# Decay masks in spare rows of the one-hot products, and weight slot 0 for few blocks only

## The chip, the cores and the metric

One core of one Trainium2 chip runs the kernel. The metric is the device time of one execution in microseconds; three runs of the kernel before gave 1845.36 to 1845.75, median 1845.67.

## The reference

A sequence of 256 tokens of width 1024 goes through two blocks of two layers each, all in float32. A layer of the first block is an FFN, a mixer and a second FFN; a layer of the second block is a hybrid layer of attention and a gated recurrence. The change lies in the mixer, whose state-space part works in chunks of 128 tokens, in both directions, for 16 heads:

```python
def ssd_chunked(x, dt, a, bm, cm):
    ...
    a_cs = jnp.cumsum(dtc * a, axis=2)
    seg = a_cs[:, :, :, None] - a_cs[:, :, None, :]
    lower = jnp.tril(jnp.ones((L, L), dtype=bool))[None, None, :, :, None, None]
    decay = jnp.exp(jnp.where(lower, seg, -jnp.inf))
    cb = jnp.einsum('bclgn,bcsgn->bclsg', cc, bc)
    y_diag = jnp.einsum('bclsg,bclsgr,bcsgrp->bclgrp', cb, decay, xd)
    ...
```

For each head, chunk and direction a 128 x 128 tile `exp(a_cs[l] - a_cs[s])` is needed, zero where s is later than l (or earlier, for the reversed direction). All other work of the change concerns the weight matrices of every projection: `x @ w` for FFNs (`w_gate`, `w_up`, `w_down`), mixers (`w_in`, `mla_w_uq`, `mla_w_ukv`, `w_out`) and hybrid layers.

## The kernel before

**Weights.** All weight matrices are cut into 586 blocks, mostly of 128 partitions x 1024 values (two 128-row pieces of the contraction, 512 columns). SyncE (SP) loads block j into a raw slot, ScalarE copies it to a rounded high part (`WH`, five buffers, j % 5), VectorE subtracts and writes the low part (`WL`) over the raw block in place. TensorE then makes three passes of fp32r products: left high by weight high, left low by weight high, left high by weight low. Products of a projection are of kind "feat" (a feature block: weights are the stationary operand, 24 products of 256 columns per block, in three thirds of 8) or "tok" (a token block: weights move, 12 products of 512 columns). The last block of a projection runs half by half. `split_of` (L1054) gives block j raw slot j % 8: slots 1 to 7 lie side by side in `RAW`/`WL`, slot 0 is a tensor of its own, `RAW0`/`WL0`, that starts at a multiple of 512 bytes, where the others don't. In its program SP waits for the end of block j - 8 before it loads block j into the slot; ScalarE's `split` (L1592) waits for the load and for the end of block j - 5, whose `WH` buffer it reuses.

**Order.** A planner in Python, the class `Order`, writes one list of phases ("block", "seg", "flip", "cum" and so on) ahead of time, and each engine runs the phases that concern it, in that order, with semaphore waits between engines. The planner has a cost for every phase (`WORK`: "P53" is 0.53 us on TensorE, A is ScalarE, V VectorE, G GpSimd) and puts phases and weight blocks where its clock says that they fit. Generators say what a phase must come after (`yield "ex", i` waits, `yield [("cum", i)]` emits).

**The mixer's decay tiles.** `cum` (TensorE L1350, ScalarE L1819, VectorE L2415) makes the cumulated logarithms by fp32 products over `DA` and `LN` and leaves them in `LBH`, 128 rows x 512: rows 0 to 15 hold one value per head with sign for the "to" side, rows 64 to 79 for the "from" side, rows 32 to 47 and 96 to 111 the low parts of the same; other rows are zero. `ex` makes exponentials from `DA`, too. `seg` (TensorE L1416) builds one PSUM bank of four 128 x 128 tiles (two directions, two heads) with five products: the mask first, the identity by `CUT` (0 or -1e30, the two directions repeated for two heads, 512 columns); then for each head a one-hot column of `TO`, repeated 128 times with step zero as the stationary operand, by 256 columns of `LBH`; then for each direction 128 columns of `LBH` by one-hot columns of `FROM`, repeated with step zero. There are 16 `seg` per mixer. ScalarE takes the exponential (`ET`), VectorE adds the directions and multiplies by C and B, and `apply` multiplies by the values with plain fp32 products. Plain fp32 products show as two matmul records each.

The heads of the mixer's attention (`sc`, `pt`, `pv`) run before; `heads()` waits for `ex`, and the tiles begin when `mo_a` of the second half is emitted. `QTQ` and `QTK` (queries and keys, at the bottom of the arena) are read last by `sc` of heads 6 and 7. `mo_var` on GpSimd is an inverse root for the attention's output norm. `cn_a` belongs to the mixer's convolution branch and stands behind the first two tiles; its PSUM bank is that of the first tile.

Of the kernel before, what the change touches and what calls it, by code (L numbers as in the profile page):

```python
# [6 lines left out]
F32 = mybir.dt.float32  # L7
F32R = mybir.dt.float32r
# [12 lines left out]
BLK = 1024  # L21
HALF = 3.1415925
STAGES = [("ffn", 0, 1), ("mix", 0), ("ffn", 0, 2), ("ffn", 1, 1), ("mix", 1), ("ffn", 1, 2),
          ("hyb", 0), ("hyb", 1)]
# [32 lines left out]
def constants():  # L57
# [22 lines left out]
    r = np.concatenate([eye, fwd, bwd, pick.reshape(128, 32)], 1)  # L80
    return np.ascontiguousarray(c, np.float32), g, r


# [70 lines left out]
class Lin:  # L154
# [88 lines left out]
class Order:  # L243
# [307 lines left out]
    def mix(self, i, l):  # L551
# [25 lines left out]
        def decay():  # L577
            yield "evict", ("sm", i)
            for x in range(4):
                yield [("decay", i, x)]  # L580
            yield "kpe", i
            for t in range(2):
                yield "lat_y", i, t
            yield [("cum", i)]
            yield [("ex", i)]

# [33 lines left out]
        def heads():  # L620
            for t in range(2):
                yield "qk_rope", i, t
            yield "ex", i
            yield "evict", ("xbc", i, 1)
            yield [("qkt", i, g) for g in range(0, 8, 2)]
            yield [("qkt", i, g) for g in range(8, 16, 2)]
            yield [("tbanks", (0, 1, 3)), ("heads", i)]
            for h in range(2):
                self.go(mla_head(h))
            yield "pv", i, 7  # L630
            yield [("mo_a", i, 1), ("tbanks", (2, 3))]
            yield [("mo_sq", i, t) for t in range(2)]
            yield [("mo_var", i, t) for t in range(2)]
            yield [("mo_y", i, t) for t in range(2)]
            yield [("flip", "mo", i, c, 2) for c in (8, 10)]
# [231 lines left out]
class Kernel:  # L867


    def __init__(self, nc, ctx, io, order):  # L870
        self.nc, self.ctx, self.io = nc, ctx, io
        self.sig = Signals(nc, ctx)
        self.order = order
        self.blocks, self.lins = order.blocks, order.lins
        self.w_at, at = [], 0
        for lin, kk, _, _ in self.blocks:
            self.w_at.append(at)
            at += 128 * len(kk) * lin.w
        self.bank, self.stats, self.stat_at = {}, {}, {}
        self.allocate()  # L880

    def fixed(self, name, shape, dt=F32):
# [21 lines left out]
    def allocate(self):  # L904
# [55 lines left out]
        self.LN, _ = mk("LN", [128, 2, 2, 128], m)  # L960
        self.MPT, m = mk("MPT", [128, 2, 2, 256], m)
        self.DA, m = mk("DA", [128, 2, 2, 128], m)
        self.DT, m = mk("DT", [128, 2, 32], m)
# [16 lines left out]
        assert x <= p2  # L980
        self.LBH, x = mk("LBH", [128, 512], p1, F32R)
        self.ET, _ = mk("ET", [128, 4, 512], 32768)
# [71 lines left out]
    def split_of(self, j):  # L1054

        lin, kk = self.blocks[j][:2]
        size = len(kk) * lin.w
        n = j % NRAW
        raw, lo = (self.RAW[:, n - 1, :], self.WL[:, n - 1, :]) if n else (self.RAW0[:, :], self.WL0[:, :])
# [60 lines left out]
class PE:  # L1120
# [229 lines left out]
    def cum(self, i):  # L1350
        k, w = self.k, self.w
        b, ps = self.tbank(("cum", i), "cum_dve", i)
        w.wait_ge(*self.at("const6", 0))
        w.wait_ge(*self.at("decay_dve", (i, 3)))
        w.wait_ge(*self.at("decay_act", (i, "ln")))
# [7 lines left out]
    def ex(self, i):  # L1363
        k = self.k
        b, ps = self.tbank(("ex", i), "ex_act", i)
        for t in range(2):
            for d in range(2):
# [48 lines left out]
    def seg(self, i, n):  # L1416
# [5 lines left out]
        w.wait_ge(*self.at("cum_dve", i))  # L1422
        w.wait_ge(*self.at("const5", 0))
        self.mm(ps, k.EYER, k.CUT.unsqueeze(2).to_broadcast([128, 2, 2, 128]), True, False)
        h0 = 8 * g + 2 * q
        for x in range(2):
            self.mm(ps[:, :, x, :], k.TO[:, h0 + x:h0 + x + 1].to_broadcast([128, 128]),
                    k.LBH[:, 256 * t:256 * t + 256].rearrange("p (d s) -> p d s", d=2), False, False)
        for d in range(2):
            m = self.mm(ps[:, d, :, :], k.LBH[:, 256 * t + 128 * d:256 * t + 128 * d + 128],  # L1430
                        k.FROM[:, h0:h0 + 2].unsqueeze(2).to_broadcast([128, 2, 128]), False, d == 1)
        m.then_inc(*self.up("seg_pe", (i, n)))
# [123 lines left out]
class Scalar:  # L1556
# [35 lines left out]
    def split(self, j):  # L1592
# [4 lines left out]
        if j == 0:  # L1597
# [4 lines left out]
            return  # L1602
        w.wait_ge(*self.at(f"raw{j % NRAW}", j))
        if j >= NSPLIT:
# [214 lines left out]
    def cum(self, i):  # L1819
# [4 lines left out]
        for t in range(2):  # L1824
            w.wait_ge(*self.at("lat_act", (i, t, "y")))
        self.act(k.LBH[:, :], ps[:, :], ACT.Copy).then_inc(*self.up("cum_act", i))

# [155 lines left out]
class Vector:  # L1983
# [431 lines left out]
    def cum(self, i):  # L2415
        k, w, e = self.k, self.w, self.e
        ps = k.PS[k.bank["cum", i]]
        w.wait_ge(*self.at("cum_act", i))
        e.tensor_tensor(k.LBH[32:64, :], ps[32:64, :], k.LBH[32:64, :].bitcast(F32), ALU.subtract)
        e.tensor_tensor(k.LBH[96:128, :], ps[96:128, :], k.LBH[96:128, :].bitcast(F32), ALU.subtract).then_inc(*self.up("cum_dve", i))  # L2420

# [323 lines left out]
class Pool:  # L2745
# [6 lines left out]
    def program(self):  # L2752
        do = {
            "setup": self.setup, "setup2": self.setup2, "rstd": self.rstd, "mix_pads": self.mix_pads,
            "lat_var": self.lat_var, "kpe": self.kpe, "qk_sum": self.qk_sum, "mo_var": self.mo_var,
            "fin_var": self.fin_var, "hyb_load": self.hyb_load,
            "hq_sum": self.hq_sum, "hb_sum": self.hb_sum, "oan_var": self.oan_var,
# [53 lines left out]
    def qk_sum(self, i, t):  # L2811
# [3 lines left out]
        for name, n in (("k", 8), ("q", 0)):  # L2815
            self.e.tensor_tensor(st[:, n:n + 8], st[:, n:n + 8], k.HM[:, 0:8], ALU.pow).then_inc(*self.up("rsqrt_pool", (name, i, t)))

    def mo_var(self, i, t):
        self.rsqrt(("mo", i, t), 8)
# [22 lines left out]
class Sync:  # L2842
# [6 lines left out]
    def program(self):  # L2849
# [10 lines left out]
        for j, (lin, kk, _, _) in enumerate(k.blocks):  # L2860
            at, size = k.w_at[j], len(kk) * lin.w
            if j < 2:
                continue
            if j >= NRAW:
                w.wait_ge(*self.at("block", j - NRAW))
            e.dma_start(k.split_of(j)[0], k.io["WALL"][at:at + 128 * size].rearrange("(p n) -> p n", p=128)).then_inc(
                *k.sig.landed(f"raw{j % NRAW}", j))
        for n in range(2):
# [30 lines left out]
def pack_small(inputs):  # L2899
# [6 lines left out]
    for name, n in ROWS:  # L2906
        for l in range(L):
# [3 lines left out]
            "ROWP": np.ascontiguousarray(np.concatenate(rows, 1)), "CST": c,  # L2911
            "CSTG": g, "CSTR": r,
            "x": np.asarray(inputs["x"]), "POSITIONS": np.ascontiguousarray(
# [30 lines left out]
```

## Time and profile before

| | us |
|---|---|
| median of three runs | 1845.67 |
| the profiled execution, its own time | 1845.08 |
| its span, first to last instruction | 1843.3 |
| TensorE busy | 1828.3 |
| VectorE busy | 1266.7 |
| ScalarE busy | 1055.9 |
| GpSimd busy | 100.5 |

The profile is one execution. TensorE's granted clock is 1.000 of full speed over it. Matmuls overlap in their pipeline and their ends are modelled, so a matmul's recorded duration is longer than its share of time; the distance from one start to the next is what it costs. The timeline merges neighbours of one kind and writes how many ("x8"). On GpSimd the records are rough. DMA queues are listed by the engine that issues: SPq for the weights, POOLq for constants.

### The profile page before, as it was taken

To read this page: it belongs to the slowest core of one execution; us is meant where nothing else is said; L and a number is where in the kernel's file an instruction comes from. 1 tells how busy PE (TensorE), PEld (TensorE's weight loads), DVE (VectorE), ACT (ScalarE), POOL (GpSimd) and SP (SyncE) were. 2 spreads that over 40 slices of the span, in tenths; PEclk is the share of its full clock that TensorE was granted. 3 is DMA by queue.
4 is the path that set the end of the run, shared out by engine and by line. 5 is a ranking of instruction groups with operands and counts; after the bars stand their busy time and mean duration, and the time that the engine had idled before them with its cause. 6 is when DMAs were issued, how large, how long until landed. Compare 5 with 4: busy or idle time off the path is not lost.

```text
span 1843.3 us, 28625 instructions
## 1 busy us (share of the span) xinstructions
PE 1828.3 (99%) x11626; PEld 1628.1 (88%) x11626; DVE 1266.7 (69%) x1944; ACT 1055.9 (57%) x1557; POOL 100.5 (5%) x85
## 2 busy tenths in 40 slices
PE   9999999999999999999999999999999999999999
PEld 9998998789998999899789998988878888887887
DVE  6764797766665665588876665687667567875755
ACT  6444767565444444576755544475776456568642
POOL 0000110000000000020000000002001000210100
PEclk9999999999999999999999999999999999999999
DMA  8555542345555556553325555554445555534553
GB/s 292 193 191 182 188 151 100 106 137 189 192 193 186 190 195 194 180 179 112 126 92 172 191 193 189 173 184 147 139 137 182 194 163 182 171 126 137 172 192 116
DMA packets 86596, 310.09 MB, mean 168 GB/s; under 512 B 9648, under 2 KB 10288, under 8 KB 86464
## 3 DMA queue, kind: packets, MB, share of 16 engines
q1 hardware_dynamic: 85680, 306.35, 50.7%
q8 instruction: 92, 1.51, 0.3%
q0 software_dynamic: 496, 1.65, 0.2%
q14 instruction: 40, 0.33, 0.1%
q10 hardware_dynamic: 288, 0.25, 0.0%
HBM read 307.16 MB, written 1.05 MB: 167 GB/s over the span
## 4 chain that ended last, share of the span: by engine, by line
PE 95%; ACT 3%; DVE 1%; issue 0%; DMA 0%; POOL 0%; SPq 0%; DVEq 0%; ACTq 0%
PE bank L1162 92%; PE bank L1159 3%; ACT PA L1579 1%; DVE PA L2686 0%; ACT MP L1579 0%; ACT WH L1579 0%; ACT L1579 0%; DVE WL L2034 0%; DMA X<-in_x_dram 0%; ACT ET L1579 0%; DVE PC L2711 0%; DVE STATS L2384 0%; ACT BZ L1579 0%; DVE BO L2676 0%; DVE X L2120 0%
## 5 line engine op out<-in xcount | busy, mean ns | idle before, releaser
L2034 DVE TENSOR_TENSOR WL<-RAW,WH 128x1024 fp32r<-128x1024 f32 x585 | 704.6, 1213 | 405.0 <-ACT WH L1579 403.4
L1579 ACT ACTIVATE WH<-RAW 128x1024 fp32r<-128x1024 f32 (+2 forms) x587 | 610.1, 1050 | 497.0 <-PE bank L1162 494.2
L1162 PE MATMUL bank<-WH,FR 128*128 128x512 f32 x1264 | 318.4, 390 | 0.0
L1162 PEld LDWEIGHTS bank<-WH,FR 128*128 128x128 f32 x1264 | 233.7, 188 | 48.4 <-issue 0.8
L1162 PE MATMUL bank<-XTH,WH 128*128 128x256 f32 x1792 | 254.4, 279 | 0.6 <-ACT XTH L1579 0.6
L1162 PE MATMUL bank<-XTH,WL 128*128 128x256 f32 x1792 | 251.9, 278 | 0.0
L1162 PE MATMUL bank<-XTL,WH 128*128 128x256 f32 x1792 | 251.1, 277 | 0.0
L1162 PEld LDWEIGHTS bank<-XTH,WH 128*128 128x128 f32 x1792 | 226.9, 188 | 1.5 <-issue 0.8
L1162 PEld LDWEIGHTS bank<-XTH,WL 128*128 128x128 f32 x1792 | 226.7, 188 | 0.0
L1162 PEld LDWEIGHTS bank<-XTL,WH 128*128 128x128 f32 x1792 | 226.0, 188 | 0.0
L1162 PE MATMUL bank<-WL,FR 128*128 128x512 f32 x632 | 173.7, 389 | 0.0
L1162 PE MATMUL bank<-WH,XTHS 128*128 128x512 f32 x576 | 165.0, 398 | 0.0
L1162 PE MATMUL bank<-WL,XTHS 128*128 128x512 f32 x576 | 160.7, 390 | 0.0
L1162 PE MATMUL bank<-WH,XTLS 128*128 128x512 f32 x576 | 160.3, 390 | 0.0
L1162 PEld LDWEIGHTS bank<-WL,FR 128*128 128x128 f32 x632 | 118.4, 188 | 24.9
L1162 PEld LDWEIGHTS bank<-WH,XTLS 128*128 128x128 f32 x576 | 108.1, 188 | 23.2
L1162 PEld LDWEIGHTS bank<-WL,XTHS 128*128 128x128 f32 x576 | 108.1, 188 | 23.1
L1162 PEld LDWEIGHTS bank<-WH,XTHS 128*128 128x128 f32 x576 | 104.3, 188 | 21.4 <-issue 2.0
L2787 POOL TENSOR_TENSOR STATS<-STATS,HALFS 128x1 f32<-128x1 f32 (+2 forms) x36 | 68.0, 1900 | 662.0 <-DVE STATS L2593 174.2
L1579 ACT ACT_TABLE_LOAD x43 | 55.2, 1283 | 3.7 <-PEq L2935 1.7
L2219 DVE SCALAR_TENSOR_TENSOR XC<-XBG,COLP,XC 128x256 f32<-128x256 f32 x96 | 46.4, 484 | 8.5 <-ACT XC L1579 5.5
L1579 ACT ACTIVATE PA<-PA,STATS 128x128 f32<-128x128 f32 x64 | 34.2, 536 | 21.6 <-DVE STATS L2692 21.6
(337 smaller groups left out, 1850.6 us busy)
## 6 DMA issues: line engine op xcount, KB each, us to landing
RAW<-in_WALL_dram SPq DMA_DIRECT2D x569, 512.0 KB, 3.3
RAW<-in_WALL_dram SPq DMA_DIRECT2D x8, 448.0 KB, 3.3
RAW<-in_WALL_dram SPq DMA_DIRECT2D x8, 256.0 KB, 2.6
X<-in_x_dram SPq DMA_DIRECT2D x4, 256.0 KB, 5.5
out_dram<-X SPq DMA_DIRECT2D x4, 256.0 KB, 2.0
ROWP<-in_ROWP_dram POOLq DMA_DIRECT2D x1, 672.0 KB, 11.0
CONSTS<-in_CST_dram POOLq DMA_DIRECT2D x1, 664.0 KB, 7.9
ROUNDED<-in_CSTR_dram POOLq DMA_DIRECT2D x1, 208.0 KB, 12.2
```

The lines of the kernel that those rows point to most:

```text
L1159: return self.e.transpose(out, in_, self.k.EYE[0:rows, 0:rows])
L1162: return self.e.matmul(out, lhs, rhs, start=start, stop=stop, skip_group_check=True)
L1579: return self.e.activation(out, in_, func, **k)
L2034: self.e.tensor_tensor(lo, raw, hi.bitcast(F32), ALU.subtract).then_inc(*self.up("lo", j))
L2219: e.scalar_tensor_tensor(o, src[:, tap:tap + 256], k.col("ssd_conv_w", l, 12 * tap + ch), o, ALU.mult, ALU.add).then_inc(*self.up("conv_dv ...
L2787: self.e.tensor_tensor(st, st, k.HM[:, 0:n], ALU.pow).then_inc(*self.up("rsqrt_pool", key))
```

## The change

Mask: the 64 free rows of the one-hot operands are filled. Each half of a mask (two -1e30 triangles) is written as a sum over 64 runs of neighbouring columns, so the one-hot matrix holds the runs and the other operand's free rows hold the cut for each run; the four one-hot products then add the mask as well, and the fifth product, the mask itself, is gone. For this the one-hot operands become real 128 x 128 matrices, one per head: `TOX` and `FROMX` (1,024 KB each), at the bottom of the arena in the room of `QTQ` and `QTK`, and the values are kept in two tiles, `LBT` (values in rows 0 to 63, cuts below) and `LBF` (cuts above, values in rows 64 to 127), the latter in the room of `DA`. A new phase `scan_load` on GpSimd loads the two matrices and the two cuts (128 KB each) in every mixer, once the scores of heads 6 and 7 and `cum` have been made. `ex` comes before `cum`, since `LBF` overwrites `DA`; `heads()` waits for `cum`. ScalarE evicts `cum` in two copies of 64 partitions.

Slots: `place_blocks` decides each block's raw slot. It collects rows of "feat" blocks of FFNs and mixers that follow each other with no other work of TensorE between them. Slot 0 goes to a block only if its last use is at least 7 blocks ago, the block isn't the last of its row, the row hasn't had it yet, and the block isn't the last of its projection; every other block takes the longest unused of slots 1 to 7. SP waits for the block that had the slot before.

```diff
+        used, self.slot, self.before = [-NRAW] * NRAW, [], []
+        for j in range(len(self.blocks)):
+            row = rows.get(j, [j])
+            if not j or (j - used[0] >= NRAW - 1 and j != row[-1] and used[0] not in row and not self.blocks[j][3]):
+                n = 0
+            else:
+                n = min(range(1, NRAW), key=lambda s: used[s])
+            self.slot.append(n)
+            self.before.append(used[n])
+            used[n] = j
...
-        n = j % NRAW
+        n = self.slot[j]
...
-            if j >= NRAW:
-                w.wait_ge(*self.at("block", j - NRAW))
+            if k.before[j] >= 0:
+                w.wait_ge(*self.at("block", k.before[j]))
...
-    "cum": "P198 A60 V140", ... "seg": "P53 A61 V90",
+    "cum": "P198 A105 V140", ... "seg": "P32 A61 V90",
...
+            yield [("ex", i)]
             yield [("cum", i)]
-            yield [("ex", i)]
...
-            yield "ex", i
+            yield "cum", i
...
-            yield [("mo_a", i, 1), ("tbanks", (2, 3))]
+            yield [("mo_a", i, 1), ("scan_load", i), ("tbanks", (2, 3))]
...
     def seg(self, i, n):
...
-        w.wait_ge(*self.at("const5", 0))
-        self.mm(ps, k.EYER, k.CUT.unsqueeze(2).to_broadcast([128, 2, 2, 128]), True, False)
+        w.wait_ge(*self.at("scan_in", i))
         h0 = 8 * g + 2 * q
         for x in range(2):
-            self.mm(ps[:, :, x, :], k.TO[:, h0 + x:h0 + x + 1].to_broadcast([128, 128]),
-                    k.LBH[:, 256 * t:256 * t + 256].rearrange("p (d s) -> p d s", d=2), False, False)
+            self.mm(ps[:, :, x, :], k.TOX[:, h0 + x, :], k.LBT[:, 256 * t:256 * t + 256].rearrange("p (d s) -> p d s", d=2),
+                    x == 0, False)
         for d in range(2):
-            m = self.mm(ps[:, d, :, :], k.LBH[:, 256 * t + 128 * d:256 * t + 128 * d + 128],
-                        k.FROM[:, h0:h0 + 2].unsqueeze(2).to_broadcast([128, 2, 128]), False, d == 1)
+            m = self.mm(ps[:, d, :, :], k.LBF[:, 256 * t + 128 * d:256 * t + 128 * d + 128], k.FROMX[:, h0:h0 + 2, :], False, d == 1)
...
-        self.act(k.LBH[:, :], ps[:, :], ACT.Copy).then_inc(*self.up("cum_act", i))
+        self.act(k.LBT[0:64, :], ps[0:64, :], ACT.Copy)
+        self.act(k.LBF[64:128, :], ps[64:128, :], ACT.Copy).then_inc(*self.up("cum_act", i))
...
+    def scan_load(self, i):
+
+        k, w, e = self.k, self.w, self.e
+        for h in (6, 7):
+            w.wait_ge(*self.at("sc_pe", (i, h)))
+        w.wait_ge(*self.at("cum_pe", i))
+        w.wait_ge(*self.at("kpe_pool", (i, 1)))
+        src = k.io["CSTX"]
+        e.dma_start(k.TOX[:, :, :], src[:, 0:2048].rearrange("p (h s) -> p h s", h=16)).then_inc(*k.sig.landed("scan_in"))
+        e.dma_start(k.FROMX[:, :, :], src[:, 2048:4096].rearrange("p (h s) -> p h s", h=16)).then_inc(*k.sig.landed("scan_in"))
+        e.dma_start(k.LBF[0:64, :], src[0:64, 4096:4608]).then_inc(*k.sig.landed("scan_in"))
+        e.dma_start(k.LBT[64:128, :], src[64:128, 4096:4608]).then_inc(*k.sig.landed("scan_in", i))
```

## Rows read from the trace of the kernel before

**Rows 1.** busy time of each engine in the whole span (page, part 1)

```profile
PE 1828.3 (99%) x11626; PEld 1628.1 (88%) x11626; DVE 1266.7 (69%) x1944; ACT 1055.9 (57%) x1557; POOL 100.5 (5%) x85
```

**Rows 2.** groups of matmuls by shape: count, busy us and mean ns

```profile
L1162 PE MATMUL bank<-ROUNDED 128*128 128x512 f32 x32 | 14.9, 465 | 0.0
```

**Rows 3.** timeline of TensorE, `seg` 7 and `seg` 11: start us, us, operation

```profile
359.63 0.48 PE L1162 MATMUL bank<-ROUNDED 128*128 128x512 f32 x1
359.95 0.40 PE L1162 MATMUL bank<-LBH,ROUNDED 128*128 128x256 f32 x2
360.18 0.38 PE L1162 MATMUL bank<-ROUNDED,LBH 128*128 128x256 f32 x2
...
368.61 0.39 PE L1162 MATMUL bank<-ROUNDED 128*128 128x512 f32 x1
368.84 0.40 PE L1162 MATMUL bank<-LBH,ROUNDED 128*128 128x256 f32 x2
```

**Rows 4.** timeline of TensorE behind `rows` of the second layer's FFN

```profile
603.05 1.19 PE L1162 MATMUL bank<-XTH,WH 128*128 128x256 f32 x8
604.08 1.10 PE L1162 MATMUL bank<-XTL,WH 128*128 128x256 f32 x8
...
605.97 1.07 PE L1162 MATMUL bank<-XTH,WH 128*128 128x256 f32 x8
```

**Rows 5.** timeline of TensorE, feature blocks 127 to 130

```profile
423.05 1.10 PE L1162 MATMUL bank<-XTH,WH 128*128 128x256 f32 x8
...
425.88 1.10 PE L1162 MATMUL bank<-XTH,WH 128*128 128x256 f32 x8
...
428.71 0.62 PE L1162 MATMUL bank<-XTH,WH 128*128 128x256 f32 x4
...
431.43 0.39 PE L1162 MATMUL bank<-XTH,WH 128*128 128x256 f32 x2
```

**Rows 6.** timeline of TensorE at the first tiles of a mixer

```profile
340.97 0.49 PE L1162 MATMUL bank<-ROUNDED 128*128 128x512 f32 x1
...
343.07 0.67 PE L1162 MATMUL bank<-CHC,CONSTS 128*32 128x256 f32 x8 [0.29 <-ACT ET L1579]
```

**Rows 7.** timeline of ScalarE at the same place

```profile
341.13 1.28 ACT L1579 ACT_TABLE_LOAD   x1 [0.65 <-PE bank L1162]
342.42 1.09 ACT L1579 ACTIVATE ET<-bank 128x512 f32<-128x512 f32 x2
```

**Rows 8.** timeline of TensorE, feature blocks 136 and 137

```profile
447.75 1.07 PE L1162 MATMUL bank<-XTH,WH 128*128 128x256 f32 x8
...
450.53 0.62 PE L1162 MATMUL bank<-XTH,WH 128*128 128x256 f32 x4
```

**Rows 9.** timeline of TensorE, token blocks 168 to 170

```profile
535.03 1.98 PE L1162 MATMUL bank<-WH,FR 128*128 128x512 f32 x8
...
537.78 2.00 PE L1162 MATMUL bank<-WH,FR 128*128 128x512 f32 x8
...
540.52 1.98 PE L1162 MATMUL bank<-WH,FR 128*128 128x512 f32 x8
```

**Rows 10.** timeline of TensorE, the last scores of a mixer

```profile
292.86 1.03 PE L1162 MATMUL bank<-QTK,QTQ 96*128 96x256 f32 x4
```

**Rows 11.** DMA issues (page, part 6): count, KB each, us to landing

```profile
RAW<-in_WALL_dram SPq DMA_DIRECT2D x569, 512.0 KB, 3.3
...
ROWP<-in_ROWP_dram POOLq DMA_DIRECT2D x1, 672.0 KB, 11.0
```

**Rows 12.** stretch, length, busy us PE, PEld, DVE, ACT, POOL; clock, DMA share, GB/s

```profile
294.60:340.90 46.30, 45.71 (x242) 36.11 (x241) 37.11 (x55) 33.72 (x50) 3.34 (x2) 1.00 0.37 123
```

**Rows 13.** costliest groups (page, part 5): ScalarE's half of the weight split

```profile
L1579 ACT ACTIVATE WH<-RAW 128x1024 fp32r<-128x1024 f32 (+2 forms) x587 | 610.1, 1050 | 497.0 <-PE bank L1162 494.2
```

**Rows 14.** instructions on tile LBH: duration min/median/max ns

```profile
L2419 DVE TENSOR_TENSOR LBH<-bank,LBH x2: 683/683/683, 245.5 to 827.6; 32x512 fp32r<-32x512 f32 x2
```

**Rows 15.** timeline of TensorE, block 274, two behind slot 0

```profile
827.60 1.10 PE L1162 MATMUL bank<-XTH,WH 128*128 128x256 f32 x8
```

More of the change, by code:

```diff
@@ L22 @@
 HALF = 3.1415925
+ON_PE = set(("warm block flip rows cn_a cn_b qkt sc pt pv cum ex xs btk cbm state fin seg apply ift chain qkf msc mse mn "
+             "as at av").split())
 STAGES = [("ffn", 0, 1), ("mix", 0), ("ffn", 0, 2), ("ffn", 1, 1), ("mix", 1), ("ffn", 1, 2),
@@ L81, in constants, with scan_constants @@
     return np.ascontiguousarray(c, np.float32), g, r
+def scan_constants():
+    ends = [(1, 2)] + [(2 * j, 2 * j + 2) for j in range(1, 63)] + [(126, 127)]
+    i = np.arange(128)
+    runs = np.stack([(i >= a) & (i <= b) for a, b in ends]).astype(np.float32)
+    s = np.zeros((2, 128, 16, 128), np.float32)
+    for x in range(2):
+        for p in (64 * x, 64 * x + 32):
+            s[x, p + i[:16], i[:16]] = 1
+        s[x, 64 * (1 - x):64 * (1 - x) + 64] = runs[:, None, :]
+    cut = np.zeros((128, 2, 2, 128), np.float32)
+    for k, (a, b) in enumerate(ends):
+        cut[64 + k, :, 0] = np.where(i < a, -1e30, 0.0)
+        cut[64 + k, :, 1] = np.where(i > b, -1e30, 0.0)
+        cut[k, :, 0] = np.where(i > b, -1e30, 0.0)
+        cut[k, :, 1] = np.where(i < a, -1e30, 0.0)
+    return np.ascontiguousarray(np.concatenate([s[0].reshape(128, 2048), s[1].reshape(128, 2048), cut.reshape(128, 512)], 1))
 class Signals:
@@ L879, in __init__, with place_blocks @@
         self.bank, self.stats, self.stat_at = {}, {}, {}
+        self.place_blocks()
         self.allocate()
+    def place_blocks(self):
+        rows, alone = {}, True
+        for phase in self.order.phases:
+            if phase[0] not in ON_PE:
+                continue
+            j = phase[1]
+            if phase[0] != "block" or self.blocks[j][0].kind != "feat" or STAGES[self.blocks[j][0].key[1]][0] == "hyb":
+                alone = True
+                continue
+            row, alone = [] if alone else row, False
+            row.append(j)
+            rows[j] = row
+        used, self.slot, self.before = [-NRAW] * NRAW, [], []
[8 more added lines that the diff above has]
+            used[n] = j
     def fixed(self, name, shape, dt=F32):
@@ L961, in allocate @@
         self.MPT, m = mk("MPT", [128, 2, 2, 256], m)
+        self.LBF, _ = mk("LBF", [128, 512], m, F32R)
         self.DA, m = mk("DA", [128, 2, 2, 128], m)
@@ L980, in allocate @@
         assert x <= p2
-        self.LBH, x = mk("LBH", [128, 512], p1, F32R)
+        self.LBT, x = mk("LBT", [128, 512], p1, F32R)
+        self.TOX, _ = mk("TOX", [128, 16, 128], 0, F32R)
+        self.FROMX, _ = mk("FROMX", [128, 16, 128], 16384, F32R)
         self.ET, _ = mk("ET", [128, 4, 512], 32768)
@@ L1352, in cum @@
         b, ps = self.tbank(("cum", i), "cum_dve", i)
-        w.wait_ge(*self.at("const6", 0))
-        w.wait_ge(*self.at("decay_dve", (i, 3)))
         w.wait_ge(*self.at("decay_act", (i, "ln")))
@@ L1363, in ex @@
     def ex(self, i):
-        k = self.k
+        k, w = self.k, self.w
         b, ps = self.tbank(("ex", i), "ex_act", i)
+        w.wait_ge(*self.at("const6", 0))
+        w.wait_ge(*self.at("decay_dve", (i, 3)))
         for t in range(2):
@@ L1602, in split @@
             return
-        w.wait_ge(*self.at(f"raw{j % NRAW}", j))
+        w.wait_ge(*self.at(f"raw{k.slot[j]}", j))
         if j >= NSPLIT:
@@ L2418, in cum @@
         w.wait_ge(*self.at("cum_act", i))
-        e.tensor_tensor(k.LBH[32:64, :], ps[32:64, :], k.LBH[32:64, :].bitcast(F32), ALU.subtract)
-        e.tensor_tensor(k.LBH[96:128, :], ps[96:128, :], k.LBH[96:128, :].bitcast(F32), ALU.subtract).then_inc(*self.up("cum_dve", i))
+        e.tensor_tensor(k.LBT[32:64, :], ps[32:64, :], k.LBT[32:64, :].bitcast(F32), ALU.subtract)
+        e.tensor_tensor(k.LBF[96:128, :], ps[96:128, :], k.LBF[96:128, :].bitcast(F32), ALU.subtract).then_inc(*self.up("cum_dve", i))
     def state_x(self, i, d):
@@ L2755, in program @@
             "lat_var": self.lat_var, "kpe": self.kpe, "qk_sum": self.qk_sum, "mo_var": self.mo_var,
-            "fin_var": self.fin_var, "hyb_load": self.hyb_load,
+            "fin_var": self.fin_var, "hyb_load": self.hyb_load, "scan_load": self.scan_load,
             "hq_sum": self.hq_sum, "hb_sum": self.hb_sum, "oan_var": self.oan_var,
@@ L2863, in program @@
                 continue
-            if j >= NRAW:
-                w.wait_ge(*self.at("block", j - NRAW))
+            if k.before[j] >= 0:
+                w.wait_ge(*self.at("block", k.before[j]))
             e.dma_start(k.split_of(j)[0], k.io["WALL"][at:at + 128 * size].rearrange("(p n) -> p n", p=128)).then_inc(
-                *k.sig.landed(f"raw{j % NRAW}", j))
+                *k.sig.landed(f"raw{k.slot[j]}", j))
         for n in range(2):
@@ L2911, in pack_small @@
             "ROWP": np.ascontiguousarray(np.concatenate(rows, 1)), "CST": c,
-            "CSTG": g, "CSTR": r,
+            "CSTG": g, "CSTR": r, "CSTX": scan_constants(),
             "x": np.asarray(inputs["x"]), "POSITIONS": np.ascontiguousarray(
```

4 rows, old and new, of the table WORK are left out of this document.

## Prediction

> **What bounds the kernel now.** I read the busy table first: TensorE is busy for 1828.3 of 1843.3 us [rows 1], so work that it need not do is time saved, unless a wait grows in its place. The profiled execution took 1845.08 us for a span of 1843.3 us; the median of the runs is 1845.67 us, 0.6 above it. I make the sum on 1845.08 and add the 0.6 at the end. The busy times of overlapping matmuls are no pace, so every price of TensorE below is a distance from start to start in its timeline.
>
> **The mask matmul goes.** Each mixer builds 16 pairs of decay tiles (`seg`), and each `seg` begins with one 512-column matmul of the mask: 32 in all [rows 2]. What it takes depends on what ran before. Behind the plain-fp32 products of `apply` it is 359.95 - 359.63 = 0.32 us; behind another `seg` 368.84 - 368.61 = 0.23 us [rows 3]. The 0.09 between them isn't the mask's: the first fp32r matmul after plain-fp32 work pays it whatever it is (behind `rows` the first third of a block takes 604.08 - 603.05 = 1.03 us [rows 4], where a third of a block at the same pace takes 2.83 / 3 = 0.94 [rows 5]). The first one-hot product will pay it instead. So I take 0.23 a tile, with 0.32 as the other end.
>
> Not all 32 count. Behind the first two tiles of a mixer stands `cn_a`, which needs the bank of the first tile and so waits for its exponential [rows 6]; and that waits for an activation-table load from 341.13 to 342.41, whatever TensorE does [rows 7]. TensorE resumes at 343.07 as before. So 28 x 0.23 = **6.4 us**; the upper end is 28 x 0.32 = 9.0.
>
> The four products that remain keep their sizes, but read real matrices where they read one column at step zero. The trace has no such pair to compare. The nearest rows are the two paces of 256-column products over real matrices, 24 to a block: 2.72 / 24 = 0.113 and 2.83 / 24 = 0.118 us [rows 5]; today's take 360.18 - 359.95 = 0.23 for two [rows 3], in between. Ends for 128 products: -0.3 and +0.6 us; I take 0.
>
> **The slots.** Today every eighth block lies in slot 0 (RAW0/WL0), 74 of 586. The new rule gives it only to a block that isn't the last of its product, in an unbroken row of feature blocks of the FFNs and mixers, not at the row's end, once per row, and at least 7 blocks after its last use; a token block is a row of its own, so its own end, and never gets it. Counted along the block order of the trace, 14 are left. What slot 0 does stands in the timeline:
>
> Feature blocks run at 2.72 or at 2.83 us. A break (`rows`, transposes) sets the slow pace, and it stays until a block in slot 0 has passed: 2.83 from 423.05, the block in slot 0 from 425.88, then 2.72 [rows 5]. At the fast pace a block in slot 0 takes 450.53 - 447.75 = 2.78, and the pace stays fast [rows 8]. A token block takes 537.78 - 535.03 = 2.75 in slot 0 and the one behind it 540.52 - 537.78 = 2.74, where 2.72 is usual [rows 9].
>
> So, first, 43 token blocks leave slot 0, each worth 0.03 to 0.05 with its follower: **1.9 us**. Second, sixteen feature blocks in rows that are fast already leave it, four in each FFN: 16 x 0.055 = **0.9 us**. Third, the cure moves. By the rule it comes one block earlier at 71 (for 72), 87 (for 88) and 311 (for 312), two at 318 (for 320); rows that had none get one at 123, 189, 259, 268 and 275, with 2, 2, 3, 3 and 1 blocks behind it; 130 for 128 and 196 for 192 lose 2 and 4. Net 10 blocks x 0.11 = **1.1 us**. Three feature blocks of the hybrid layers leave slot 0 without gain, under 0.1 against. Together **3.8 us**.
>
> A rule of the Trainium skill speaks against this part. "SBUF — State Buffer", section "Who interferes with whom", gives TensorE two independent read ports, one for the moving operand and one for weights, and says that it never waits for anyone. By it the place of a weight block sets no pace and the part is worth 0. The trace disagrees: the same 24 products take 2.72, 2.78 or 2.83 us [rows 5, 8].
>
> **The scan load.** Four DMAs from POOL's queue, 2,304 KB per mixer, go out when the scores of heads 6 and 7 are done, at 293.9 [rows 10]. Behind them on POOL stands `mo_var` alone, which needs sums of heads that come later still; no weight load is in that queue. The first reader is `seg` 0 at 340.97 [rows 6], 47 us later. Bounds by the nearest loads: 512 KB in 3.3 us, and 672 KB in 11.0 us among others [rows 11], so 15 to 38 us. The DMA engines are 37% busy in that stretch [rows 12]. Hidden: 0. Without that cover each late us would be one of TensorE's, in both mixers. Weight loads that share the engines have room: ACT's split waited 494.2 us for TensorE to release a buffer [rows 13], not for data.
>
> **Seven slots in place of eight.** A load is then released by the end of block j-7. It lands 3.3 us later [rows 11], and the split waits for the end of block j-5 anyway, 2 x 2.72 = 5.4 us after the release. 0, by that margin of 2.1 us.
>
> **`ex` ahead of `cum`, and a copy in two.** The same products swap places. ACT copies twice 64 partitions, beside TensorE. On VectorE the two subtractions of `cum`, 0.68 us each [rows 14], come nearer to the rope of queries and keys, for which the heads' first transposes wait. Ends: 0, and 2 x 1.4 = 2.8 us if they push it in both mixers; the work ahead of that rope stays the same, so 0.
>
> **The planner** books `seg` at P32 in place of P53 and may interleave the output blocks otherwise. Each switch from plain fp32 to fp32r costs 0.09 [rows 3]; ten more or fewer per mixer are 1.8 us, either way. I take 0.
>
> **Sum.** 6.4 + 3.8 = 10.2; 1845.08 - 10.2 = 1834.9, on the scale of the median **1835.5 us**.
>
> **Rivals.**
>
> *The cure misses.* At block 272, behind `cum`, slot 0 did not cure: two blocks later a third still takes 1.10 us busy [rows 15], as at the slow pace, where the fast one has 1.07 [rows 5]. Today the next try comes 8 blocks later; with one try per row a miss lasts. Each FFN has one row of some 40 blocks, so a miss there costs 35 x 0.11 = 3.8 us. One gives 1839.3; from three on the kernel is slower than before (11.4 against 10.2), and four give 1850.7. Against it: behind `rows` it worked even at the head of a row (1.07 at 605.97 [rows 4]), and the four new places are inside theirs, as at 425.88. One miss 8%, more 3%, mostly all four, since they are alike.
>
> *The place of a block sets no pace:* what looks like the slot's doing comes from something else and stays: 1845.7 - 6.4 = 1839.3. For it: that one uncured case. 5%. The rule of the Trainium skill above would have it so.
>
> *The mask's time comes back as waits* for the exponentials or VectorE's two products per tile: 1845.7 - 3.8 = 1841.9. For it: the first pair of tiles does so today [rows 6, 7]. Against: each later pair has a weight block of 2.7 us between its `seg` and its `apply`. 6%.
>
> *The entry cost goes with the mask:* 9.0 in place of 6.4, 1832.9. 10%.
>
> *The load lands late:* from under 2,304 KB / 47 us = 49 KB per us on; the slower row moves 61. Ten us late in each mixer give 1855. 2%.
>
> **How the numbers follow.** The forecast has the remaining 66%. The range reaches below to the lost entry cost with a kind interleaving and quicker cures, 1830, and above to one miss with slow one-hot products, 1840.5; that leaves out less than 2 in 10. A measurement of this kernel can tell 0.2%, 3.7 us, from no change. Slower by more: four misses or a late load, 4%. Within: two or three misses, or the waits with a little more against them, 6%. Faster: 90%.
>
> **What would show it.** Right: the row of 32 mask matmuls is gone; from a `seg`'s first product to the next work it is 0.23 us shorter; TensorE's pause ahead of `cn_a` grows by 0.46; token blocks take 2.72 in unbroken rows; each FFN's long row turns from 2.83 to 2.72 once and never shows 2.78. Wrong: an FFN row at 2.83 to its end; TensorE waiting for the load at `seg` 0; one-hot products above 0.118; new waits for the exponentials; many blocks elsewhere in the order.

## The result, and the profile after

The kernel after takes 1848.30 us (median of 20, 1846.93 to 1850.96), the kernel before beside it 1845.49: a ratio of 1.0013, 95% interval 1.0007 to 1.0019. I had forecast 1835.5, in a range from 1830.0 to 1840.5. The time rose by 2.8 us where 10.2 were to go.

The profiled execution of after took 1848.81 us. Its first weight block starts at 9.84 us, that of before at 7.81; executions of one kernel differ by that much at the start (those of before lie at about 1845.2 or about 1847.4), so traces are compared from the first weight block on.

The parts of the change show as forecast. Of the kernel after: part 1 of the page (beside [rows 1]), the groups that replace the products over `LBH`, and DMA issues (columns as in [rows 11]):

```profile
PE 1824.0 (99%) x11594; PEld 1624.4 (88%) x11594; DVE 1266.7 (69%) x1944; ACT 1056.9 (57%) x1559; POOL 102.9 (6%) x93
...
L1211 PE MATMUL bank<-LBT,TOX 128*128 128x256 f32 x64 | 15.0, 316 | 0.2
L1211 PE MATMUL bank<-FROMX,LBF 128*128 128x256 f32 x64 | 12.7, 280 | 0.0
...
TOX<-in_CSTX_dram POOLq DMA_DIRECT2D x2, 1024.0 KB, 5.7
FROMX<-in_CSTX_dram POOLq DMA_DIRECT2D x2, 1024.0 KB, 7.6
```

The 32 mask matmuls of [rows 2] are gone, the scan load has landed 10 us after its first issue, where the first reader comes 50 us after it, and TensorE is busy 4.3 us less. Yet the span is 3.7 longer: what TensorE no longer does it now waits. Its waits that grew, first in after, then in before (us in total, times, longest):

```profile
PE bank L1211 <- DVE ET L2503: 3.6, 4, 1.1
...
PE bank L1208 <- ACT XS L1626: 2.0, 2, 1.0
...
PE bank L1211 <- ACT ET L1626: 1.0, 2, 0.5
...
PE bank L1162 <- ACT ET L1579: 0.6, 2, 0.3
...
PE bank L1159 <- ACT XS L1579: 0.5, 2, 0.3
```

In before TensorE waited for `ET` 0.6 us in all and never for VectorE's half of it. Cut into stages (from the start of a stage's first weight block in TensorE's timeline to that of the next stage), the six FFN and hybrid stages of after are 2.54 us shorter together, and the mixers longer: 216.13 to 218.82 and 216.49 to 218.04.

The reason stands in the list of phases. In each mixer the planner sorted everything behind `cum` and `ex` anew. Here are TensorE's phases of the decay tiles in both kernels (B is a weight block of `w_out`):

```
before: ... cn_b cn_b apply2 apply3 seg4 seg5 B apply4 seg6 apply5 seg7 B apply6 seg8 apply7 seg9
        cn_b cn_b apply8 apply9 seg10 seg11 B ... apply13 seg15 B flip flip apply14 apply15
after:  ... cn_b cn_b apply2 apply3 seg4 seg5 apply4 seg6 apply5 seg7 cn_b cn_b apply6 apply7
        seg8 seg9 B B apply8 seg10 apply9 seg11 B ... apply13 seg15 apply14 flip flip apply15
```

After spends a `w_out` block earlier, ahead of `seg` 0, and so has none between `seg` 5 and `apply` 4, nor behind `seg` 15. The timeline of TensorE in after, at `seg` 5 and at the end of the tiles, with the clock there (start, us, operation; in brackets idle time and what ended it; the windows have length, busy us of PE, PEld, DVE, ACT, POOL, granted clock, DMA share, GB/s):

```profile
359.42 0.40 PE L1211 MATMUL bank<-LBT,TOX 128*128 128x256 f32 x2
359.66 0.40 PE L1211 MATMUL bank<-FROMX,LBF 128*128 128x256 f32 x2
361.19 0.66 PE L1211 MATMUL bank<-XS,ET 128*128 128x64 f32 x4 [1.13 <-DVE ET L2503]
...
382.41 0.48 PE L1211 MATMUL bank<-LBT,TOX 128*128 128x256 f32 x2
382.73 0.40 PE L1211 MATMUL bank<-FROMX,LBF 128*128 128x256 f32 x2
383.82 0.66 PE L1211 MATMUL bank<-XS,ET 128*128 128x64 f32 x4 [0.69 <-DVE ET L2503]
385.46 1.94 PE L1208 MATMUL bank<-CONSTS,XS 128*128 128x128 f32 x8 [0.98 <-ACT XS L1626]
387.20 0.96 PE L1211 MATMUL bank<-XS,ET 128*128 128x64 f32 x4
...
384.00:386.00 2.00, 1.01 (x7) 0.91 (x8) 1.90 (x4) 2.00 (x3) 0.00 (x0) 0.81 0.01 2
386.00:388.00 2.00, 2.00 (x12) 2.00 (x10) 1.74 (x4) 1.66 (x5) 0.54 (x1) 0.50 0.03 8
```

At 361.19 `apply` 4 starts 1.3 us late: the tile must pass ScalarE's exponential and two products on VectorE first, and no block covers that. At 383.82 and 385.46 it happens twice in a row, and then the granted clock falls from 2.4 to 1.2 GHz: the eight transposes take 1.74 us from start to start, where they take 0.90 at 2.4 GHz (e11, below). The mean granted clock of after was below 1.000 in 19 of its 20 executions; before never shows that.

### The profile page after: what moved, and what is told of

Same layout as the page of the kernel before. It is cut to its first block, busy times and chain, and to the rows that moved or that the text cites. A ratio compares the mean times of both kernels' runs of the same rounds, so it can differ in the third digit from the quotient of the medians.

```text
span 1847.0 us, 28571 instructions
## 1 busy us (share of the span) xinstructions
PE 1824.0 (99%) x11594; PEld 1624.4 (88%) x11594; DVE 1266.7 (69%) x1944; ACT 1056.9 (57%) x1559; POOL 102.9 (6%) x93
## 4 chain that ended last, share of the span: by engine, by line
PE 90%; DVE 5%; ACT 4%; issue 1%; DMA 0%; POOL 0%; SPq 0%; DVEq 0%; ACTq 0%
PE bank L1211 87%; PE bank L1208 3%; DVE WL L2082 1%; ACT PA L1626 1%; ACT WH L1626 1%; DVE XC L2267 1%; DVE PA L2734 0%; DVE STATS L2386 0%; ACT MP L1626 0%; ACT L1626 0%; ACT ET L1626 0%; DMA X<-in_x_dram 0%; DVE XBG L2215 0%; DVE PC L2759 0%; DVE STATS L2432 0%
## 5 line engine op out<-in xcount | busy, mean ns | idle before, releaser
L1211 PEld LDWEIGHTS bank<-WH,XTHS 128*128 128x128 f32 x576 | 104.3, 188 | 20.9 <-issue 2.0
```

The lines of the kernel that those rows point to most:

```text
L1211: return self.e.matmul(out, lhs, rhs, start=start, stop=stop, skip_group_check=True)
```

## The experiments

Twelve kernels ran. The table has their medians beside the kernel before on the same chip, and from each trace the length against before's trace: the two mixers, the other six stages, and all from the first weight block on.

| kernel | median | before | mixers | others | sum |
|---|---|---|---|---|---|
| after | 1848.30 | 1845.49 | +2.69, +1.55 | -2.54 | +1.70 |
| e1 old order | 1840.49 | 1845.65 | -2.34, -2.16 | -2.18 | -6.68 |
| e2 swap alone | 1857.42 | 1845.65 | +5.84, +4.83 | -0.11 | +10.56 |
| e3 slots alone | 1843.57 | 1845.65 | -0.08, -0.50 | -2.10 | -2.68 |
| e4 mask alone | 1843.06 | 1845.65 | -0.93, -1.81 | +0.77 | -1.97 |
| e5 block up | 1852.07 | 1846.85 | +4.88, +3.61 | -2.64 | +5.85 |
| e6 bookings | 1847.48 | 1846.85 | +1.07, +1.34 | +0.50 | +2.91 |
| e7 no slot 0 | 1855.90 | 1846.85 | -1.94, -1.89 | +13.27 | +9.44 |
| e8 idle product | 1838.18 | 1846.85 | -2.28, -2.25 | -2.27 | -6.80 |
| e9 block early | 1845.07 | 1845.55 | +1.23, +0.89 | -2.57 | -0.45 |
| e10 mask and idle product | 1841.75 | 1845.55 | -2.17, -1.87 | +0.41 | -3.63 |
| e11 tail | 1846.00 | 1845.55 | +0.96, +0.55 | -2.17 | -0.66 |
| e12 all aligned | 1859.12 | 1845.55 | -0.47, -1.59 | +16.67 | +14.61 |

### The order against the parts

`e1_old_order`: after, with `Order` as before, and then

```diff
+        for i, st in enumerate(stages):
+            if st[0] == "mix":
+                self.phases.remove(("ex", i))
+                self.phases.insert(self.phases.index(("cum", i)), ("ex", i))
```

> The kernel after, with the list of phases of the kernel before: the planner books and sorts as before (cum ahead of ex, seg P53, cum A60), and ex is then moved up to stand just ahead of cum. Masks, loads and slots are those of after. Theory: the swap of ex and cum made the planner sort the rest of each mixer otherwise, and that order costs what the change was to bring; with the old order the mask and the slots bring their 6.4 and 3.8 us, so 1845.5 - 10.2 = 1835.3 (1834 to 1838). Rival: the new operands, their load or the slots cost it themselves, and the order is a bystander: about 1848, as after.

Measured: 1840.49, ratio 0.9968 (0.9956 to 0.9981). The rival falls: with the old order the same masks, loads and slots are faster than before. But 5.2 us came, not 10.2. The trace has 6.68; it is of the one execution of five whose mean granted clock was 1.000, and the fastest. What is missing from the forecast is taken apart below.

`e2_swap_alone`: before, with the two generator lines of the diff (`ex` yielded ahead of `cum`, `heads` waiting for `cum`) and the bookings of after.

> The kernel before, with ex ahead of cum for the planner and with the bookings of after (seg P32, cum A105), so that TensorE has the order of after with the old masks and the old slots. Theory: the order alone costs 1848.3 - 1835.3 = 13 us, so 1858.5 (1855 to 1861); waits for ET between seg and apply show as in after. Rival (the parts cost it, not the order): 1845.5.

Measured: 1857.42, ratio 1.0059 (1.0047 to 1.0072). The order and the bookings cost 11.8 us, by the trace all of it in the mixers. Part of it is the clock: the mean was below 1.000 in all five executions, with the old masks still in place. After lies 9.1 below this kernel, so in the new order the parts bring most of their 10.2: by the traces 6.4 in the mixers and 2.4 elsewhere.

`e6_booking`: before, `"seg": "P32 A61 V90"` and `"cum": "P198 A105 V140"` alone. Of TensorE's phases only `apply` 14 moves; on ScalarE and VectorE a few `split` and `fin` phases move too.

> The kernel before with the bookings of after alone (seg P32 for P53, cum A105 for A60), cum still ahead of ex. The list then differs from that of before in one place per mixer: apply 14 stands ahead of the two flips of ys. Theory (the swap re-sorts the mixer, not the bookings): 1845.6, within 0.5. Rival (the planner's bookings cost it, as the prediction put that step): 5 us or more above.

Measured: 1847.48, ratio 1.0007 (0.9998 to 1.0016). The ratio can't tell that from no change; by the trace the mixers are 1.07 and 1.34 longer, so 0 was too low. `apply` 14 itself doesn't wait here, since a block still stands between `seg` 15 and it. The flips behind it do, and so does the block behind `apply` 15, as TensorE's timeline in mixer 2 shows:

```profile
965.57 0.55 PE L1162 MATMUL bank<-XS,ET 128*128 128x64 f32 x4
966.67 1.06 PE L1159 MATMUL bank<-CONSTS,XS 128*128 128x128 f32 x8 [0.55 <-ACT XS L1579]
967.57 0.56 PE L1162 MATMUL bank<-XS,ET 128*128 128x64 f32 x4
968.35 2.43 PE L1162 MATMUL bank<-WH,FR 128*128 128x512 f32 x8 [0.22 <-ACT FR L1579]
```

The bookings cost about 2.4 us in the order of before, not 5. If they cost as much in the new order, the swap has the rest of e2's 10.67 in the mixers, 8.3.

Why a swap of two neighbours sorts a mixer anew can be read by replaying the planner. In before it places `cum`, three weight blocks with splits and a convolution between them, and then `ex`; swapped, `ex` and `cum` stand back to back, and the evictions and convolutions behind them fall into other gaps. When the first `xs` is placed the planner's clock for VectorE stands at 302.4 where it stood at 308.0, so `xs` goes one weight block earlier, and every choice behind it shifts. No engine's work had changed.

### Which gap costs what

`e5_block_up`: after, with the first of the two blocks behind `seg` 9 moved up to `apply` 4.

> The kernel after with one edit of its list per mixer: the first of the two wout blocks behind seg 9 moves up to stand between seg 5 and apply 4. In after, seg 5 and seg 15 with apply 14 hold TensorE up for want of ET, 1.3 and 2.1 us per mixer more than in the kernel with the old order. Theory (a tile's chain over ScalarE and VectorE needs a weight block as cover): the 1.3 us at seg 5 go, in both mixers, so 2.6 less than after: 1845.7. Rival (VectorE is the bound of the stretch, a block that is moved only moves the wait): 1848.3, as after.

Measured: 1852.07, 3.8 slower than after. Neither answer came. The timeline of TensorE shows why:

```profile
359.29 0.40 PE L1217 MATMUL bank<-FROMX,LBF 128*128 128x256 f32 x2
360.87 2.33 PE L1217 MATMUL bank<-WH,FR 128*128 128x512 f32 x8 [1.19 <-ACT FR L1632]
...
370.56 2.34 PE L1217 MATMUL bank<-WH,FR 128*128 128x512 f32 x8 [1.19 <-ACT FR L1632]
```

The moved block waits itself, for its left operand `FR`: ScalarE writes it behind the same exponentials. A block covers a wait only if its own operands are there. Of the `w_out` blocks four are ready when the tiles begin; after has used two of them by `seg` 0, before only one.

`e9_block_early` tests just that on the fast kernel (e8, below): one ready block more is spent ahead of the last two `fin`, one less stands between `seg` 5 and `apply` 4.

> The kernel with the old order and the idle product in seg 9 (1838.2), and one edit of its list per mixer: the weight block between seg 5 and apply 4 is spent earlier, as the swap made the planner do: three blocks in place of two stand ahead of the last two fin, and none between seg 5 and apply 4 (the blocks keep their own order). The moving of a wout block that lacked its left operand, in the run with the block moved up, showed only where that operand comes from. Theory (the stretch of decay tiles lives on weight blocks whose left operands are ready, and has just enough of them): TensorE waits 1.3 us at seg 5 in both mixers as in after, 1838.2 + 2.6 = 1840.8; if the clock falls too, 1842 to 1843. Rival (the place of single blocks makes no difference, the swap costs by something else): 1838.2.

Measured: 1845.07 (1842.86 to 1846.30), 6.9 above e8. `apply` 4 is 1.3 us late in both mixers; the timeline of TensorE in the first:

```profile
356.83 0.40 PE L1223 MATMUL bank<-LBT,TOX 128*128 128x256 f32 x2
357.07 0.40 PE L1223 MATMUL bank<-FROMX,LBF 128*128 128x256 f32 x2
358.60 0.66 PE L1223 MATMUL bank<-XS,ET 128*128 128x64 f32 x4 [1.13 <-DVE ET L2517]
...
363.74 0.66 PE L1223 MATMUL bank<-XS,ET 128*128 128x64 f32 x4 [0.31 <-DVE ET L2517]
...
367.67 1.86 PE L1223 MATMUL bank<-XS,ET 128*128 128x64 f32 x8 [0.21 <-DVE ET L2517]
```

More followed than I had priced: waits of 0.3 and 0.2 us at two later `apply`, and the clock at 1.2 GHz in both mixers of this trace (granted 0.51 from 370 to 372 and 0.56 from 952 to 954), though the idle product of e8 is in place. Against e8 each mixer is 3.1 to 3.5 us longer, for one block in another place. The supply of ready blocks is shown to be a cause.

`e11_tail`: after with `"seg": "P60 A61 V90"`, which on TensorE only puts the two flips ahead of `apply` 14; on ScalarE and VectorE some `split` and `fin` phases move as well.

> The kernel after with seg booked at P60 in place of P32: its list is that of after but for one place per mixer, where the flips of ys stand ahead of apply 14 again. Theory (apply 14 straight behind seg 15 waits for its ET, and the flips behind it): the 1.1 to 1.3 us per mixer that the bookings alone cost go, 1848.3 - 2.4 = 1845.9. Rival (apply 14 waits for the same ET wherever it stands): 1848.3.

Measured: 1846.00, 2.3 below after, as expected: in mixer 1, where after's clock fell, 1.7 us and in mixer 2 1.0. The mean granted clock is 1.000 in all ten executions, where after had it in one of 20. That the sum fits so well is in part luck: its 1.1 to 1.3 us per mixer came from e6, where it isn't `apply` 14 that waits, and some of mixer 1's 1.7 us is the clock. The flips still wait, but `apply` 14 finds its tile ready (TensorE's timeline):

```profile
381.10 0.40 PE L1211 MATMUL bank<-FROMX,LBF 128*128 128x256 f32 x2
382.88 1.06 PE L1208 MATMUL bank<-CONSTS,XS 128*128 128x128 f32 x8 [1.39 <-ACT XS L1626]
383.78 1.00 PE L1211 MATMUL bank<-XS,ET 128*128 128x64 f32 x8
```

### The masks alone, and TensorE's clock

`e4_mask_alone`: e1 with `n = j % NRAW` in place of the rule for slots.

> The kernel after with the order of before and slots j % 8: masks in the spare rows alone. Theory: 6.4 us less, 1839.1; with the entry cost of the fp32r products gone too 1836.5. Rival (the load, real matrices as operands or waits for the exponentials take it back): 1843 to 1848.

Measured: 1843.06, ratio 0.9985 (0.9976 to 0.9994): 2.6 where 6.4 were expected. The tiles do lose their 14 x 0.22 us per mixer. But the mean granted clock was below 1.000 in 9 of 11 executions, which before never shows, and in the profiled one it falls once, in mixer 1 behind `cn_b`, at about 369.0, as TensorE's timeline and two windows show:

```profile
366.70 1.45 PE L1212 MATMUL bank<-RS,SPREAD 32*128 32x256 f32 x4
368.20 1.89 PE L1212 MATMUL bank<-XS,ET 128*128 128x64 f32 x8
369.85 0.77 PE L1212 MATMUL bank<-LBT,TOX 128*128 128x256 f32 x2
370.42 0.63 PE L1212 MATMUL bank<-FROMX,LBF 128*128 128x256 f32 x2
...
368.00:370.00 2.00, 1.81 (x10) 1.53 (x10) 1.57 (x5) 0.01 (x1) 0.00 (x0) 0.76 0.00 0
370.00:372.00 2.00, 2.00 (x10) 2.00 (x10) 0.28 (x1) 0.66 (x2) 0.00 (x0) 0.50 0.00 0
```

From 369.85 to 370.42 two products take 0.57 us; where the clock holds, as in e8 below, they take 368.90 - 368.58 = 0.32. That mixer saves 0.9 us less than the other, where the clock holds. So I put one mask product back, in `seg` 9, ahead of that place, as work whose result is overwritten:

```diff
+        if n == 9:
+            self.mm(ps, k.EYER, k.CUT.unsqueeze(2).to_broadcast([128, 2, 2, 128]), True, False)
```

`e8_idle_product` is e1 with it:

> The kernel after with the old order, and in each mixer the mask's product put back into seg 9 alone, as an idle product that the next one overwrites. There TensorE waits 0.3 us at apply 8 since the masks went, and in one execution of the kernel with masks alone its granted clock then fell to 1.2 GHz from 368.5 to 372.3. Theory (TensorE's work is not missed there, ET comes late): the product is free, 1840.5 or, if it keeps the clock at 2.4 GHz, about 1839 with mean granted clocks of 1.000. Rival (each product costs its 0.22 wherever it stands): 0.4 more, 1840.9, clocks as before.

Measured: 1838.18 (1838.09 to 1840.56), ratio 0.9962 (0.9949 to 0.9974), and the mean granted clock is 1.000 in all five executions; in e1 it was so in one of five. The product costs 0.23 us where it stands, and +0.06 and -0.09 us over the two mixers against e1's trace, in which the clock held as well. This is the lowest median of all; whether it is below e1's is not clear, since the two intervals overlap. The same place in it:

```profile
366.06 1.45 PE L1215 MATMUL bank<-RS,SPREAD 32*128 32x256 f32 x4
367.44 1.34 PE L1215 MATMUL bank<-XS,ET 128*128 128x64 f32 x8
368.58 0.48 PE L1215 MATMUL bank<-LBT,TOX 128*128 128x256 f32 x2
368.90 0.39 PE L1215 MATMUL bank<-FROMX,LBF 128*128 128x256 f32 x2
...
368.00:370.00 2.00, 1.98 (x15) 1.84 (x15) 0.76 (x4) 0.67 (x2) 0.00 (x0) 1.00 0.00 0
370.00:372.00 2.00, 2.00 (x11) 1.64 (x10) 1.93 (x6) 1.21 (x3) 0.00 (x0) 1.00 0.00 0
```

`e10_mask_idle` is e4 with the same two lines:

> The kernel with masks alone (old order, slots j % 8), with the mask's product put back into seg 9 as an idle product. With masks alone the mean granted clock was below 1.000 in most executions and the time 1843.06. Theory (less work on TensorE between cn_b and seg 11 lets the granted clock fall; the idle product keeps it): granted clock 1.000, and 1 to 2 us less, 1841.5. Rival (the clock falls by chance or for another reason): 1843, clocks as before.

Measured: 1841.75 (ratio 0.9975, 0.9965 to 0.9985), 1.3 below e4, and 1.000 in 9 of 10 executions; by the traces mixer 1, where e4's clock fell, is 1.2 us shorter. Twice, then, the idle product kept the clock, and here it gained time.

It is no sure means, and the missing products no sure trigger. In e7 below, without the idle product, the clock was 1.000 in three of four executions; in e12, with it, in two of four. In e12's trace it fell in mixer 1 at about 372.3, again behind `cn_b`, `apply` 8 and 9, though TensorE is busy for 1.97 of the 2.00 us before:

```profile
371.74 0.48 PE L1216 MATMUL bank<-LBT,TOX 128*128 128x256 f32 x2
372.06 0.40 PE L1216 MATMUL bank<-FROMX,LBF 128*128 128x256 f32 x2
...
370.00:372.00 2.00, 1.97 (x12) 1.50 (x13) 1.84 (x5) 0.51 (x1) 0.00 (x0) 1.00 0.01 2
372.00:374.00 2.00, 2.00 (x11) 1.81 (x11) 0.84 (x3) 1.26 (x3) 0.00 (x0) 0.59 0.00 0
```

What sets the moment of a fall stays open.

### The slots

`e3_slots_alone`: before with `place_blocks`, `slot` and `before`.

> The kernel before with the new rule for raw slots alone. Theory: 3.8 us less by the prediction, 2.5 to 3.8 by the stages of the two traces outside the mixers, so 1841.7 to 1843. Rival (the place of a block sets no pace): 1845.5.

Measured: 1843.57, ratio 0.9987 (0.9978 to 0.9996). The gain is real; its size is taken apart below.

`e7_no_slot0`: e1 with `if not j:` as the rule.

> The kernel after with the old order, and slot 0 for block 0 alone; all other blocks take turns in slots 1 to 7. Theory (a feature row stays at 2.83 until a block in slot 0 has passed): the 146 FFN blocks and 12 mixer blocks that take 2.72 in the kernel with the old order take 2.83, 158 x 0.11 = 17.4 us, so 1840.5 + 17 = 1857.5. Rival (the Trainium skill, page SBUF - State Buffer, section Who interferes with whom: weights have a read port of their own and TensorE waits for no one, so the place of a block sets no pace): 1840.5.

Measured: 1855.90, 15.4 above e1 (17.7 above e8, which ran beside it). All FFN rows stay slow to their ends, as these lines of two neighbouring blocks show (compare [rows 5]); 166 whole FFN blocks take 2.83. Only the places of the blocks changed, so the prediction's rival, by which the place sets no pace, falls. The rule of the Trainium skill ("SBUF — State Buffer", section "Who interferes with whom"), that TensorE never waits on anyone, doesn't foresee this; whether TensorE waits here for another engine's access, no run shows.

```profile
446.68 1.10 PE L1215 MATMUL bank<-XTH,WH 128*128 128x256 f32 x8
...
449.50 1.10 PE L1215 MATMUL bank<-XTH,WH 128*128 128x256 f32 x8
```

`e12_all_aligned`: e8 with `self.top += -self.top % 512` ahead of `WL` and `RAW`.

> The kernel with the old order and the idle product (1838.2), with all eight raw slots at multiples of 512 bytes; so far slots 1 to 7 lie 192 bytes behind one and slot 0 alone on one. Theory A (what slot 0 does comes from its address): every block then does as one in slot 0, token blocks 2.75 in place of 2.72 and fast feature blocks 2.78: 256 x 0.03 + 158 x 0.055 = 16 us more, less up to 5 us where rows are cured at once, 1849 to 1855. Theory B (it comes from its being another tensor, or from its distance to the others): 1838.2. The rule of the Trainium skill (SBUF - State Buffer, Who interferes with whom) would have 1838.2 too.

Measured: 1859.12, 20.9 above e8, 4 to 10 more than theory A had. Two of its four executions have a mean granted clock below 1.000, the profiled one among them. The edit moves slots 1 to 7 by 320 bytes and nothing else, since slot 0 began at the next multiple already. Every block now does about as one in slot 0: feature blocks in the FFNs' long rows take 449.67 - 446.89 = 2.78 from the second on, to the end of their rows, token blocks 2.77.

```profile
446.89 1.07 PE L1216 MATMUL bank<-XTH,WH 128*128 128x256 f32 x8
...
449.67 1.07 PE L1216 MATMUL bank<-XTH,WH 128*128 128x256 f32 x8
...
538.42 2.00 PE L1216 MATMUL bank<-WH,FR 128*128 128x512 f32 x8
...
541.20 2.00 PE L1216 MATMUL bank<-WH,FR 128*128 128x512 f32 x8
```

So it is the address of a block that sets the pace, not its being in another tensor.

## Why the prediction was wrong

**The step that failed is the planner's, with the swap's.** I took 0 for `ex` ahead of `cum`, since the same products swap places on the engines, and 0 with 1.8 us either way for the planner, pricing only switches between plain fp32 and fp32r. On the engines the swap does cost nothing: in e1, where `ex` also stands just ahead of `cum`, no phase of a mixer in front of `seg` 2 takes 0.12 us more than in before but block 276, which has another slot. In the list, swap and bookings together cost 8.7 us (after against e1, the two mixers: 5.03 + 3.71), and what they cost is cover: ready work between a tile's `seg` and its `apply`. I also named the wrong edit: I tied the re-sorting to the booking of `seg` at P32, which has about 2.4 us of it. Two of the prediction's signs of being wrong came true: new waits for the exponentials, and blocks elsewhere in the order.

**The rival that came closest was dismissed by that same step.** "The mask's time comes back as waits" had 6% because "each later pair has a weight block of 2.7 us between its `seg` and its `apply`". That was read from the list of before and is lost in after at `seg` 5 and `seg` 15. Even in before it fails for pairs 3, 8 and 9, which have only `cn_b` ahead of their `apply`; at 8 and 9 part of the mask's time came back (below). Its price, 1841.9, was too low as well: it let the waits take the mask's time and no more, where the new order took 8.7 us, the fall of the clock in mixer 1 of this trace included.

**The mask: right where it was priced, too high in the sum.** `seg` falls from 12.83 to 9.81 us per mixer in e1, 3.0 where I had 3.2; the first two tiles of a mixer gain nothing, as forecast; the first one-hot product behind `apply` pays the entry cost (382.73 - 382.41 = 0.32 for two products against 359.66 - 359.42 = 0.24 behind a `seg`, in after's lines above), so that rival falls; real matrices take 0.117 us a product on average, within the bounds (whose upper end for 128 products is 0.4 us by its own rows, 0.118 against today's 0.115, not 0.6). But of the 6.0 us some 1.8 return in the old order too: 0.30 between `apply` 8 and `apply` 9 in each mixer, and in the two blocks around the flips of `ys` 0.42 in mixer 1 and 0.83 in mixer 2. And the granted clock falls in most executions of e1 and e4, which no step had.

**The slots: 2.7 us where I had 3.8, by e3's trace.** Token blocks gain 1.87, as forecast (1.9). Feature blocks gain less: my count of cured blocks was 10 net, and the trace has 15 cured and 10 lost, 5 net, 0.55 us in place of 1.1; two of the forecast cures failed: behind blocks 87 and 275, new places of slot 0 one block ahead of a row's end, the next block took 2.90 and 2.95, and 276 is one of the ten. Blocks 0 to 4 are 0.5 slower in this execution, and slower in those of e1 and e4 too; that belongs to its start. The sixteen fast blocks gave their 0.05 each.

**Right:** the scan load is hidden (landed 40 us before its first reader; that rests on the traces, no run took the cover away), seven slots in place of eight cost no wait, and no long row of an FFN missed its cure.

The sum again, from the traces: mask -6.0 with 1.8 of it back, and slots -2.7, make -6.9, where e1 has -6.7; the order adds 8.4 over all stages, and that makes after's +1.7. By the medians after is 2.8 above before; a trace is one execution, and the starts and the number of falls of the clock differ between executions.

## What to carry to other kernels

Where a program sorts the work, an edit that moves one entry is an edit of the whole list behind it: replay the list before pricing the edit, and price each gap by the chain that runs in it and the ready work that covers it, since a block whose own operand is late covers nothing. When a part's gain doesn't arrive, hold the order fixed and make the change alone; here that turned +2.8 us into -5.2. Work that is taken from TensorE where it waits anyway saves nothing, and can go with a fall of its clock: look at the granted clock of every execution, and where it falls try an idle product, which kept it in e8 and e10, though not in all of e12.

## What the runs showed that I had not expected

- The place of a weight block sets TensorE's pace by its address: in the FFNs' long rows whole feature blocks take 2.72 or 2.83 us 192 bytes behind a multiple of 512, and with all blocks on a multiple 2.77 to 2.78; token blocks 2.72 against 2.77. One block on a multiple takes such a row from 2.83 to 2.72, and without any the row stays at 2.83. What of the address does it stays open.
- With one product of 0.22 us per tile taken out, the mean granted clock was below 1.000 in 9 of 11 executions; in the traced one it fell to 1.2 GHz behind the two products of `cn_b` on 32 rows (four records) and a pause of 0.3 us. One idle product of 0.23 us in `seg` 9 kept it at 1.000 in 14 of 15 executions of two kernels, but in only two of four of a third (e12).
- The order at the tiles' end went with the clock too: after has a mean of 1.000 in one of 20 executions, e11, which moves two flips and a few phases of ScalarE and VectorE, in ten of ten.
